# Expert unit of a two-block model: the first turn of activations behind the whole second gate and up half, half of the next unit's row turns behind it

## The reference

```python
return (jax.nn.silu(xi @ w1[e]) * (xi @ w3[e])) @ w2[e]     # first block
g, u = jnp.split(t @ w_gu, 2, axis=-1)                       # second block
return (jax.nn.silu(g) * u) @ w_dn
```

## Time and profile before

| what | us |
|---|---|
| runs | 4598.0, 4605.4, 4610.13 |
| median | 4605.4 |
| span of the profiled execution | 4600.3 |
| time of the profiled execution beside its span | not given |
| PE busy in the span | 3623.1 (79%) |
| expert stage of the first layer, from 1330 | 503 |
| expert stage of the second block, from 3794 | 697 |

### The profile page before, as it was taken

How to read it: one execution, slowest core, us unless ns; L and a number is a source line. 1 busy time by engine, 2 the same in 40 slices (tenths; PEclk the granted TensorE clock), 3 DMA queues, 4 the chain that set the end, 5 groups by cost and what they waited for, 6 DMA issues and landing times. The chain is left out here.

```text
span 4600.3 us, 65334 instructions
## 1 busy us (share of the span) xinstructions
PE 3623.1 (79%) x24112; PEld 2301.4 (50%) x24113; DVE 1334.3 (29%) x2393; ACT 816.0 (18%) x1867; POOL 875.4 (19%) x911
## 2 busy tenths in 40 slices
PE   4989998999768888599489884996658759999990
PEld 2468966896344444134345441441435326666660
DVE  2533443343320001311311003007545341111115
ACT  1422242221101111100111111100015002222220
POOL 0034412442011111000111111005200013333333
PEclk7999998999869999799699996998668779999995
DMA  6840001002259999532499996430020218998885
GB/s 248 207 127 1 1 19 37 1 1 75 78 210 418 408 408 377 220 129 92 165 396 392 415 420 246 156 120 19 0 67 1 110 43 317 371 358 299 337 317 180
DMA packets 148939, 895.17 MB, mean 195 GB/s; under 512 B 56120, under 2 KB 57402, under 8 KB 102587
## 3 DMA queue, kind: packets, MB, share of 16 engines
q1 hardware_dynamic: 95260, 764.21, 43.0%
q10 hardware_dynamic: 31908, 78.71, 4.8%
q0 software_dynamic: 21632, 50.37, 3.3%
HBM read 833.97 MB, written 81.26 MB: 199 GB/s over the span
## 5 line engine op out<-in xcount | busy, mean ns | idle before, releaser
L1620 PE MATMUL ps<-weight_ring,moe_xT 128*64 128x128 f32 (+1 forms) x2656 | 462.6, 329 | 66.7 <-DMA weight_ring<-in_w_dram 65.7
L1620 PE MATMUL ps<-moe_spare,moe_xT 128*64 128x128 f32 (+1 forms) x2528 | 448.2, 333 | 75.4 <-issue 75.4
L1622 PE MATMUL ps<-moe_spare,moe_xT 128*64 128x128 f32 (+1 forms) x2592 | 468.3, 337 | 0.0
L1622 PE MATMUL ps<-weight_ring,moe_xT 128*64 128x128 f32 (+1 forms) x2656 | 463.1, 330 | 0.0
L1767 DVE TENSOR_TENSOR moe_act<-moe_sg,ps 64x128 f32<-64x128 f32 (+1 forms) x344 | 118.8, 345 | 1082.4 <-ACT moe_sg L1721 1082.4
L1620 PEld LDWEIGHTS ps<-weight_ring,moe_xT 128*64 128x64 f32 x2656 | 327.3, 142 | 210.2 <-DMA weight_ring<-in_w_dram 82.7
L1620 PEld LDWEIGHTS ps<-moe_spare,moe_xT 128*64 128x64 f32 x2528 | 315.5, 143 | 198.7 <-issue 137.6
L1589 POOL COPY moe_xg<-moe_xin 64x1024 f32<-64x1024 f32 x172 | 177.5, 1032 | 1190.7 <-PE ps L1603 898.3
L1622 PEld LDWEIGHTS ps<-weight_ring,moe_xT 128*64 128x64 f32 x2656 | 326.5, 142 | 0.0
L1622 PEld LDWEIGHTS ps<-moe_spare,moe_xT 128*64 128x64 f32 x2592 | 325.0, 143 | 0.0
L1721 ACT ACTIVATE moe_sg<-ps 64x128 f32<-64x128 f32 (+1 forms) x344 | 108.0, 314 | 947.9 <-PE ps L1622 910.5
(11 more groups left out here) (573 smaller groups left out, 5815.5 us busy)
## 6 DMA issues: line engine op xcount, KB each, us to landing
weight_ring<-in_w_dram SPq DMA_DIRECT2D x96, 2048.0 KB, 10.1
moe_spare<-in_w_dram SPq DMA_DIRECT2D x92, 2048.0 KB, 10.5
weight_ring<-in_w_exp_gu_dram SPq DMA_DIRECT2D x32, 2048.0 KB, 10.8
moe_spare<-in_w_exp_gu_dram SPq DMA_DIRECT2D x32, 2048.0 KB, 9.1
expert_rows<-moe_y ACTq DMA_DIRECT2D x344, 128.0 KB
moe_spare<-in_w_exp_dn_dram SPq DMA_DIRECT2D x16, 2048.0 KB, 11.8
weight_ring<-in_w_exp_dn_dram SPq DMA_DIRECT2D x16, 2048.0 KB, 12.5
expert_rows<-delta_o SPq DMA_DIRECT2D x1, 25088.0 KB, 130.0
```

Of the source, the lines that this page charges most:

```text
L1620: nc.tensor.matmul(m.ps[0:UR, half, 0:W], xT[:, k, :], gate[:, k, cols], start=(k == 0), stop=(k == KD - 1))
L1622: last = nc.tensor.matmul(m.ps[UR:P, half, 0:W], xT[:, k, :], up[:, k, cols], start=(k == 0), stop=(k == KD - 1))
```

## The change

In `unit`, the second half of gate and up runs to its end before the first turn of activations. `turn_x(u + 1, 0)`, the first half of the next unit's row turns, follows that turn directly; it stood behind the first down product. No semaphore, buffer or instruction of another engine changes. Line numbers behind the place fall by one.

```diff
                 pe.wait_ge(acted[0], u + 1)
                 gate_and_up(gate, up, 0, 0, KD)
                 pe.wait_ge(acted[1], u + 1)
-                gate_and_up(gate, up, 1, 0, KD // 2)
+                gate_and_up(gate, up, 1, 0, KD)
                 turn_a(u, 0)
-                gate_and_up(gate, up, 1, KD // 2, KD)
+                turn_x(u + 1, 0)
                 weights_there(2)
                 pe.wait_ge(s.y_copied, u + 1)
                 down_product(u, down, 0)
-                turn_x(u + 1, 0)
                 turn_a(u, 1)
                 turn_x(u + 1, 1)
                 after_hi = pe.value_load(r.start[0:1, bass.ds(e + 2, 1)], min_val=0, max_val=r.units)
```

## The result

In 15 runs each, the changed kernel takes 4583.7 us at the median and the kernel before 4610.8; the ratio is 0.9946, 95% interval 0.9934 to 0.9958, so 25 us less. The prediction had 50 us less, 4555, in a range up to 4582. The sign was right, the size was twice what came, and the measured time lies just above the range. The kernel before has a median 5.4 above that of the three runs from which the prediction started; that shifts the time forecast, not the gain.

A forecast was written before the change was run, and what follows sets the result against it. In the 64-expert stage PE was taken to set the pace, waiting at L1613 for VectorE's product. A gain of 55 us, less 5 for transfers, plus 0 in the first block, gave 4605.4 - 50 = 4555 us, range 4543 to 4582.

The forecast's parts named there:

- What bounds the stage, and which wait goes: 64-expert stage: PE hardly waits for weights; its 50.6 us of waits at L1613 for VectorE's product are what the change removes.
- late units: 64-expert units with a late product: 7.9 us more of waits lie there, of which 1.5 in all stays.
- the first block's layers: Expert stages of the first block's two layers: waits for weights swallow any effect, so 0 us, within 3 us each.
- First turn at 3.58: Ordinary 64-expert unit: first turn starts 3.58 us behind the unit's start, its product ready at 3.23, the 0.44 wait gone.
- I take 0.55: First turn to first down product in a 64-expert unit: 0.55 us, as in the second turn's trip, against 1.10 before.
- 0.96 instead of 1.26: First down product to second turn in a 64-expert unit: 0.96 us, since the row turns no longer stand between.
- second trip kept at 0.55: Second turn to second down product in a 64-expert unit: stays 0.55 us.
- Transfers take 5 us: 64-expert stage: weight transfers take back 5 us of the 55 us gain, with bounds of 0 and 36.
- rival 3: 64-expert stage: turns standing together lower PE's clock, 74 us more at 0.876, so slower at 4624 us; chance 0.06.
- Rival 2: 64-expert units: the trip from turn to down product takes 1.05 instead of 0.55, so no gain, 4605 us; chance 0.06.
- Rival 1: 64-expert stage: transfers take back most of the gain, 36 us, leaving 19 and a time of 4586 us; chance 0.15.

The follow-up runs named there:

- E3: Changed kernel with the waits for down weights and the copied result set ahead of the row turns; ratio 0.9936 to the kernel before.
- E2: Kernel before with only the four row turns moved ahead of the first down product, first turn left in place; ratio 1.0051, 24 us slower.
- E4: Changed kernel with all eight row turns between the first turn and the first down product; ratio 0.9948 to the kernel before.
- E1: Changed kernel with the row turns back behind the first down product, so only the first turn is moved; ratio 0.9976 to the kernel before.
- E5: Changed kernel with half of each weight load of the 64-expert stage left out; ratio 0.9912 to the kernel before.
- E8: Changed kernel with down-weight and result waits ahead of the row turns, and down weights loaded before the second expert's gate and up; ratio 0.9894 to the kernel before.

## Why the prediction was half right

*What bounds the stage, and which wait goes.* Right. PE sets the pace, the wait at L1613 went from 50.6 to 0.6, the product is ready in the ordinary unit, the late units fit, and the first block's layers kept their length.

*First turn at 3.58.* Right: 3.59.

*"I take 0.55" for turn to down product.* This is the step that failed, with 0.68. I read the second turn's trip and carried it over. Two things were different at the new place. The second turn stood behind row turns, inside a burst, and began to count at its short form; the first turn opens a burst, with no wait ahead of it (272 instead of 223 ns at L1613, ACT's copy 0.31 behind it instead of 0.26 to 0.28). And its down product has three waits, one of them a separate instruction: 0.09, shown by E3. Together they make about the 0.13.

*"0.96 instead of 1.26" and the second trip kept at 0.55.* Off by 0.05 and 0.04. A product that follows turns starts slower than one that follows gate products (E2, E4), and the second turn, now directly behind the down product, opens a burst (E1, where it stays inside one, has 0.53). I priced the moved instructions at their spacing inside a burst and forgot that the edit changes who stands at the edges. The three terms, 0.13, 0.05 and 0.04, are 0.22 per unit, 21 us over the stage, where the forecast of 50 is missed by 21 (by the turns' span) to 25 (by the times).

*The two halves.* The prediction added them up as separate savings. Alone they give -11 us (E1) and +24 (E2), together -25. The turn's move opens a gap of 0.41 behind it; the rows' move fills that gap, and keeps the number of bursts at two because both edits join the turns to one group. The rows' move alone is a loss, and the turn's move alone is worth less than half of the pair.

*Transfers take 5 us.* Right in kind, somewhat small. In the changed kernel's profile they take 7.9 (E5), where PE's waits account for 6.4. Most of the rest is the clock. The two waits with their down products, and the windows around the longer one (columns as in the earlier trace rows):

```profile
3962.30 1.08 PE L1631 MATMUL ps<-weight_ring,moe_aT 128*64 128x512 f32 x4 [2.26 <-DMA weight_ring<-in_w_exp_dn_dram]
...
4436.16 1.98 PE L1631 MATMUL ps<-weight_ring,moe_aT 128*64 128x512 f32 x4 [4.09 <-DMA weight_ring<-in_w_exp_dn_dram]
```

```profile
4426.00:4434.00 8.00, 6.00 (x80) 4.46 (x78) 1.27 (x3) 1.58 (x5) 2.17 (x3) 1.00 1.04 366
4434.00:4442.00 8.00, 5.84 (x49) 3.30 (x51) 0.69 (x1) 0.82 (x2) 2.02 (x3) 0.79 1.00 398
```

PE stood for 4.09 us, the granted clock fell from its upper level, and the four down passes took 1.98 instead of 1.08. That unit lasted 12.2 us, 5.4 more than an ordinary one, of which 4.1 is the wait. Behind the wait of 2.26 the passes still took 1.08. The prediction named the stretch of 4405 to 4465 and the end of the stage; the longer wait is there. The shorter one is in the stretch of 3925 to 3990, in which it let PE live from what was loaded ahead. And it did not see that the order of loads, not the rate, made them (E8).

*Rivals.* The clock did not fall with the turns in groups. It is 0.99 over the window of the stage; what is missing to 1.00 stands at its start, where PE had just waited 18.6 us for GpSimd's first rows, as before the change, and behind the longer wait:

```profile
3800.00:3809.00 9.00, 7.23 (x72) 6.97 (x72) 0.29 (x1) 0.87 (x2) 4.07 (x6) 0.55 0.24 74
3809.00:4434.00 625.00, 600.72 (x7470) 431.48 (x7467) 115.95 (x274) 144.67 (x457) 197.30 (x273) 1.00 0.94 355
```

So rival 3's 4624 is out: ten turns per unit, in groups of five among products, did not lower the clock here. The rule that the prediction took from the Trainium skill, "TensorE: Matmul & The Clock Gate", Part 4: PE-mode transpose, that a transpose does not count as activity for the clock in the way products do, is neither borne out nor refuted by that; no run has turns alone. Rival 2 is nearest: the trip did become a wait, but of 0.16, not 0.5. Rival 1's 36 us given back are out as a mechanism, though its time, 4586, happens to be near the measured one.

*The sum again*, by what was measured: 0.27 for an ordinary unit times 97 is 26; late units 8 to 10 (what E1 and E5 save beyond the ordinary unit); transfers -8: 26 to 28, and 25 to 29 was measured.

## What to carry to other kernels

Before moving short instructions of PE, count the changes between kinds (turns and wide products) in the loop before and after: here one burst more cost 0.27 us per unit with no wait in sight, and one gap filled was worth as much. A trip through another engine, read off one place of the trace, did not hold at another where a different instruction stood ahead of it and more waits behind it. And once the engine that set the pace is faster, look at which transfer lands last before its use, and reorder the loads before looking for bandwidth.

## What the runs showed of the hardware beyond expectation

- The same turn of 64 by 64 lasts 221 to 223 ns inside a burst and 272 ns as its first directly behind products (243 where PE had waited ahead of it, as in the kernel before), and a down product of four passes has its first pass 0.05 us longer behind turns (1.08 against 1.03 us for the four). The weight load of a product starts 0.11 us ahead of it behind other products, and together with it behind turns (E2).
- A down product that waits for one semaphore starts 0.05 us behind ACT's copy (E3); with three, one of them waited for by a separate instruction, 0.13.
- After 4.09 us of waiting, the granted clock went to its lower level for part of the next 8 us (mean 0.79), and the wait cost a third more than its length: 5.4 us. Behind the wait of 2.26 us the four down passes took the usual 1.08.
